# Vector 5 of layer 0 weighed by VectorE, routing in fewer operations, and one expert's share of a gate quarter placed in the second gather buffer

## The reference, cut to what matters

```python
c_act = jax.nn.silu(c)
for layer in range(DEPTH):
    mod = c_act @ w_ada[layer] + b_ada[layer]
    sh1, sc1, g1, sh2, sc2, g2 = jnp.split(mod[:, None, :], 6, axis=-1)
    h = rmsnorm(x, mix_norm_g[layer]) * (1.0 + sc1) + sh1
    ...
g_idx = jnp.argmax(g_logits, axis=-1).astype(jnp.int32)
top_v, top_i = lax.top_k(e_logits, TOP_K)
e_w = jax.nn.softmax(top_v, axis=-1) * g_w[:, None]
...
def expert_block(args):
    xb, e = args
    return (jax.nn.silu(xb @ w_gate[e]) * (xb @ w_up[e])) @ w_down[e]
```

## Time and profile before

| | us |
|---|---|
| median of 3 runs | 1225.13 (1224.36 to 1225.23) |
| the profiled execution's own time | 1224.53 |
| its span, first to last instruction | 1222.8 |
| TensorE busy, VectorE busy | 885.8, 359.5 |
| mean granted TensorE clock | 0.877 of full speed |
| moved by DMA over the span | 490.06 MB, mean 401 GB/s |

### The profile page before, as it was taken

One profiled execution on the slowest core, in us unless ns is written; L12 is line 12 of the kernel. 1 busy time (PEld: TensorE's weight loads), 2 busy tenths in 40 slices (PEclk: granted clock), 3 DMA queues, 4 the chain that ended last, 5 costly groups with the idle time before them and its releaser, 6 DMA issues.

```text
span 1222.8 us, 14486 instructions
## 1 busy us (share of the span) xinstructions
PE 885.8 (72%) x5988; PEld 428.3 (35%) x5988; DVE 359.5 (29%) x900; ACT 169.7 (14%) x400; POOL 23.1 (2%) x67
## 2 busy tenths in 40 slices
PE   6999998647474756656699999976566665665647
PEld 5867453222231212121278554532121212121212
DVE  3298545121111111111124587521111111202111
ACT  1124331000000000000033253400000000000000
POOL 1001100000000000000000100000000000000000
PEclk9999999878887868787899999998787878877888
DMA  9999999999999999999996849799999999999997
GB/s 346 396 401 408 410 406 423 424 428 427 428 428 428 429 428 429 428 427 428 401 409 256 336 191 379 291 419 428 428 428 428 428 428 429 428 429 429 427 426 290
DMA packets 64249, 490.06 MB, mean 401 GB/s; under 512 B 5664, under 2 KB 8113, under 8 KB 39616
## 3 DMA queue, kind: packets, MB, share of 16 engines
q1 hardware_dynamic: 61680, 486.56, 96.1%
q10 hardware_dynamic: 2512, 2.69, 0.6%
HBM read 488.18 MB, written 1.05 MB: 400 GB/s over the span
## 4 chain that ended last, share of the span: by engine, by line
DMA 51%; PE 40%; DVE 3%; SPq 3%; ACT 1%; issue 1%; POOL 0%; DVEq 0%; ACTq 0%
PE psum L1663 40%; DMA weight_ring<-in_moe_w_down 18%; DMA weight_ring<-in_moe_w_gate 17%; DMA weight_ring<-in_moe_w_up 14%; SPq L496 2%; DMA weight_ring<-in_w_ada 1%; SPq L525 1%; DVE h_or_mix_T L1138 0%; PE psum L1759 0%; DVE h_or_mix_T L1404 0%; ACT phase_region L912 0%; DVE phase_region L1614 0%; ACT phase_region L1039 0%; DVE phase_region L1108 0%; DVE phase_region L1225 0%
## 5 line engine op out<-in xcount | busy, mean ns | idle before, releaser
L1663 PE MATMUL psum<-weight_ring,h_or_mix_T 128*32 128x512 f32 (+1 forms) x2240 | 381.7, 705 | 228.0 <-DMA weight_ring<-in_moe_w_gate 134.8
L1663 PEld LDWEIGHTS psum<-weight_ring,h_or_mix_T 128*32 128x32 f32 (+1 forms) x2240 | 119.2, 135 | 472.5 <-issue 470.0
L1663 PE MATMUL psum<-weight_ring,ada_partials 128*32 128x512 f32 (+1 forms) x1088 | 140.2, 671 | 81.1 <-DMA weight_ring<-in_moe_w_down 76.0
L1663 PE MATMUL psum<-phase_region 128*128 128x128 f32 (+5 forms) x824 | 155.4, 350 | 4.3 <-DVE x_tokens L1389 1.3
L1663 PEld LDWEIGHTS psum<-phase_region 128*128 128x128 f32 (+2 forms) x824 | 99.6, 188 | 77.4 <-issue 57.2
L1663 PE MATMUL psum<-h_or_mix_T,weight_ring 128*128 128x256 f32 (+1 forms) x528 | 115.0, 376 | 2.9 <-DVE h_or_mix_T L1138 2.7
L1663 PEld LDWEIGHTS psum<-h_or_mix_T,weight_ring 128*128 128x128 f32 x528 | 96.6, 190 | 20.3 <-issue 4.4
L1663 PEld LDWEIGHTS psum<-weight_ring,ada_partials 128*32 128x32 f32 x1088 | 40.7, 125 | 170.9 <-issue 161.2
L1458 DVE TENSOR_TENSOR phase_region<-psum,gate_rows 128x512 f32<-128x512 f32 x28 | 19.4, 692 | 207.7 <-PE psum L1663 207.7
L1447 DVE SCALAR_TENSOR_TENSOR ada_partials<-phase_region,psum 128x512 f32<-128x512 f32 x16 | 16.8, 1051 | 211.3 <-PE psum L1663 211.3
L1442 DVE SCALAR_TENSOR_TENSOR phase_region<-phase_region,psum 128x512 f32<-128x512 f32 x16 | 11.0, 687 | 228.0 <-ACT phase_region L945 228.0
(11 more groups left out here) (217 smaller groups left out, 469.9 us busy)
## 6 DMA issues: line engine op xcount, KB each, us to landing
weight_ring<-in_moe_w_up SPq DMA_DIRECT2D x64, 2048.0 KB, 20.1
weight_ring<-in_moe_w_gate SPq DMA_DIRECT2D x62, 2048.0 KB, 20.2
weight_ring<-in_moe_w_down SPq DMA_DIRECT2D x60, 2048.0 KB, 19.8
weight_ring<-in_w_ada SPq DMA_DIRECT2D x10, 3072.0 KB, 20.4
weight_ring<-in_odd_w_in SPq DMA_DIRECT2D x6, 2048.0 KB, 23.2
weight_ring<-in_w_ada SPq DMA_DIRECT2D x10, 1024.0 KB, 22.6
weight_ring<-in_w_ada SPq DMA_DIRECT2D x4, 2048.0 KB, 17.7
weight_ring<-in_even_w_in SPq DMA_DIRECT2D x3, 2048.0 KB, 21.1
```

Source lines behind the costliest of these rows:

```text
L1663: return pe.matmul(out_, lhsT, rhs, start=first, stop=last, **kw)
```

## The change

Three parts, in both layers unless said otherwise.

**Vector 5.** `modulation_sums(5, ...)`, the copy and `gate_join(5)` go. VectorE weighs the eight row blocks of the slab (`weigh_gate`, one operation of 128x1024 each) in five places of its program, and TensorE adds over the partitions with two matmuls (`add_gate_rows`) after the router's. SyncE's waits follow. Around it the convolution's centring, squares and sums are moved forward on VectorE, ScalarE and TensorE. Layer 0 only.

**Routing.** The comparisons read the integer indices directly, without a cast ahead of them; two one-hot operations and an addition become one operation of twice the width, which TensorE reads as it is, in twice as many matmuls.

**The share.** Gate quarter 1 is loaded for three experts. The fourth's share (512 KB) goes to `ASIDE`, which is `XT[:, 1]`, once the router's matmuls are done; the quarter of a down matrix (512 KB) whose place this leaves free is loaded right behind, and only the other 1.5 MB wait for `first_quarters`.

```diff
+        ASIDE = XT[:, 1, :, :].rearrange("p k q -> p (k q)")
...
+                kept = WIDE - 1 if (k, half) == (0, 1) else WIDE
+                sp.dma_start(by_quarter(EXTRA if first else region(n, half))[:, 0:kept],
+                             gate_src[L, :, 0:kept, at:at + QUARTER]).then_inc(extra_in if first else filled(n, half), 16)
...
                 if L == 0:
+                    sp.wait_ge(gate_weighted, KD // 2)
+                    load_first(3, 1)
                     sp.wait_ge(out_half, 1)
                     load_first(2, 1)
-                    sp.wait_ge(ada_half, 1)
-                    load_first(3, 1)
+                    sp.wait_ge(gate_weighted, KD)
+                    load_first(4, 0)
                     sp.wait_ge(wout_done, 4)
                     load_first(3, 0)
-                    sp.wait_ge(ada_summed, sums_by(5))
-                    load_first(4, 0)
...
+                n, rows = MOE0[L] + 4, by_quarter(region(MOE0[L] + 4, 1))
+                sp.wait_ge(logits_done, L + 1)
+                sp.dma_start(ASIDE, gate_src[L, :, WIDE - 1, QUARTER:2 * QUARTER]).then_inc(extra_in, 16)
+                sp.dma_start(rows[:, KF - 1], down_src[L, :, 1, (KF - 1) * D:KF * D]).then_inc(filled(n, 1), 16)
                 sp.wait_ge(first_quarters, 3 * L + 1)
-                load_unit(L, 4, 1, 0)
+                sp.dma_start(rows[:, 0:KF - 1], down_src[L, :, 1, 0:(KF - 1) * D].rearrange("p (k n) -> p k n", k=KF - 1)
+                             ).then_inc(filled(n, 1), 16)
...
+            def add_gate_rows():
+
+                pe.wait_ge(gate_weighted, KD)
+                for half in range(2):
+                    ins = mm(PS[:, (6, JOIN_BANK[5])[half], :], ONES[:, :], GATE_ROWS[:, half * HALF:(half + 1) * HALF], True, True)
+                ins.then_inc(gate_summed, 1)
...
-            modulation_sums(5, 0, KD // 2)
             pe.wait_ge(conv_out, 1)
...
-                    modulation_sums(5, KD // 2, KD)
+                    add_gate_rows()
                     keep_warm(1, 5)
                 else:
-                    pe.wait_ge(router_ready, 2 * L + 2)
                     add_rows(11)
-                    keep_warm(1, 8)
+                    keep_warm(1, 5)
...
+                        if part == 1:
+                            pe.wait_ge(extra_in, 16 * (4 + 2 * L))
+                            experts[-1] = ASIDE
...
-                if L == 0:
-                    gate_join(5)
-                else:
-                    keep_warm(1, 9)
+                keep_warm(1, 8)
```

More of the change, by code:

```diff
@@ L383, in landed @@
             return 16 * sum(home(m, h) == home(n, half) for m in range(n + 1) for h in range(2)
-                            if (m, h) <= (n, half) and not (m in MOE0 and h == 0))
+                            if (m, h) <= (n, half) and not (m in MOE0 and h == 0)
+                            for part in range(2 if (m - 4 in MOE0 and h == 1) else 1))
         def occupant(n):
@@ L1255, in _, with weigh_gate @@
             ins.then_inc(conv_centred, 1)
-            take_modulation(4)
+            floor_logs(3)
             dve.wait_ge(conv_squared, 1)
             add_blocks(CSQ)
+            take_modulation(4)
+            def weigh_gate(lo, hi):
+                s = slab_index("ada", 5)
+                for k in range(lo, hi):
+                    if k == 0:
+                        dve.wait_ge(slab_in[SPOT[s]], landed(s, 0))
+                        ins = v.tensor_scalar(GATE_ROWS, wide(s)[:, k, :], CCOL[:, 1, k:k + 1], None, ALU.mult)
+                    else:
+                        if k == ADA_FIRST:
+                            dve.wait_ge(rest_in[SPOT[s]], landed(s, 1))
+                        dve.wait_ge(gate_weighted, k)
+                        ins = v.scalar_tensor_tensor(out=GATE_ROWS, in0=wide(s)[:, k, :], scalar=CCOL[:, 1, k:k + 1],
+                                                     in1=GATE_ROWS, op0=ALU.mult, op1=ALU.add)
+                    ins.then_inc(gate_weighted, 1)
+            weigh_gate(0, 1)
             dve.wait_ge(conv_rstd, 1)
@@ L1355, in moe @@
                 dve.wait_ge(rank_done, L + 1)
-                for s in range(2):
-                    ins = v.tensor_tensor(ONEHOT[:, s, :, :], ONEHOT[:, s, :, :],
-                                          PS[:, 7, P:P + TB * NE].rearrange("p (t n) -> p t n", t=TB), ALU.mult)
-                link(ins)
+                dve.wait_ge(onehot_ready, L + 1)
+                link(v.tensor_tensor(ONEHOT[:, :, :, :], CHOSEN[:, :, :, :],
+                                     PS[:, 7, P:P + TB * NE].rearrange("p (t n) -> p t n", t=TB).unsqueeze(1)
+                                     .broadcast_to([P, 2, TB, NE]), ALU.mult))
                 link(v.tensor_reduce(RANK.rearrange("p t s -> p s t"), ONEHOT[:, 0:2, :, :], AX.X, ALU.add))
@@ L1977, in moe @@
                 ins.then_inc(logits_done, 1)
+                pe.wait_ge(router_ready, 2 * L + 2)
                 if L == 0:
[L1979 removed]
+                    add_gate_rows()
                     keep_warm(1, 5)
                 else:
[L1982 removed]
                     add_rows(11)
[L1984 removed]
+                    keep_warm(1, 5)
                 pe.wait_ge(onehot_ready, L + 1)
[L1987 to L1993 removed]
+                for t in range(TB):
+                    at = slice(P + t * NE, P + (t + 1) * NE)
+                    for s in range(2):
+                        ins = mm(PS[:, 7, at], BEFORE[:, :], CHOSEN[:, s, t, :], s == 0, s == 1 and t == 0,
+                                 skip_group_check=True)
+                for s in range(2):
+                    ins = mm(PS[:, 7, at], ALL[:, :], CHOSEN[:, s, 0, :], False, s == 1, skip_group_check=True)
+                ins.then_inc(rank_done, 1)
+                for s in range(2):
+                    for t in range(TB):
+                        ins = mm(PS[:, 0, 0:NE], ALL[:, :], CHOSEN[:, s, t, :], s + t == 0, s + t == 2,
+                                 skip_group_check=True)
+                ins.then_inc(counted, 1)
                 def gather(buf, done):
@@ L2049, in widen_first @@
                         pe.wait_ge(arrived, land)
+                        experts = [w[:, e] for e in range(WIDE)]
+                        if part == 1:
+                            pe.wait_ge(extra_in, 16 * (4 + 2 * L))
+                            experts[-1] = ASIDE
                         for k in (2 * part, 2 * part + 1):
@@ L2053, in widen_first @@
                                 ins = mm(PS[e * SLOT:(e + 1) * SLOT, 0, :], xt[:, k, e * SLOT:(e + 1) * SLOT],
-                                         w[:, e, k % 2 * F:(k % 2 + 1) * F], n == 0 and k % 2 == 0, n == 3 and k % 2 == 1,
+                                         experts[e][:, k % 2 * F:(k % 2 + 1) * F], n == 0 and k % 2 == 0, n == 3 and k % 2 == 1,
                                          skip_group_check=True)
```

79 lines of the change are left out of this document (33 added, 46 removed).

## The result

The changed kernel's median is 1232.53 us (1229.47 to 1235.87, 7 executions), that of the kernel before in the same comparison 1225.13: a ratio of 1.0058, with a 95% interval of 1.0048 to 1.0067. It is slower by 7.4 us. The forecast was 1228.1, slower by 3.0; the time lies outside its range. The profiled execution took 1230.23 (span 1228.4), 5.7 more than the profiled one of before; so the trace shows 5.7 of the 7.4.

The account below looks back on a forecast made before the run. The DMA engines were taken to bound the kernel, with layer 0's queue all but dry at the release and a gap in layer 1. Layer 0 +4.9 and layer 1 -1.9 gave +3.0 on 1225.13, 1228.1 us; range 1224.5 to 1230.5.

Parts of the forecast that it names:

- layer 0's share: Layer 0: share lands at 180.1 behind a full queue, first quarter waits and runs at half clock; costs 4.9 us.
- the fifty matmuls: Layer 0, TensorE: 32 records fewer at 146.24 and again at 167.85, part of vector 5's change, costed at nothing.
- Which resource sets the end, and the share's place in the queue: DMA engines set the end; layer 0's share, queued in order, lands at 180.1, so the release is 6.1 us later.
- The rival that the share overtakes what is ahead of it: Layer 0: share lands by about 176 and costs nothing, layer 1 gains 1.9; time 1222.9, chance 0.17.
- Less the 1.2 us of bytes already moved, the rest of layer 0's stream runs 4.9 us later: Layer 0: release 6.1 us later, credited 1.2 us for the early down quarter; bounds 3.4 and 6.1.
- the rival of a second gap: Layer 0: later refills of the first quad come 1.2 us closer to the queue's end, credit lost; 1229.3, chance 0.07.
- Vector 5 and the reordering "at nothing": Layer 0 before the first quarter: costs nothing, since the DMA backlog until 178 or later covers several microseconds either way.
- the first dent: Layer 0, 177 to 180: DMA at 289 of 429 GB/s over 3 us; closing it gains 1.0 us at most.
- Layer 1: Layer 1: routing 0.7 us earlier plus 1.2 us of down quarter moved into the gap; gains 1.9, bounds 0.4 to 2.3.

Follow-up runs that it names:

- the shifted changed kernel: Changed kernel plus 25 two-column matmuls on TensorE in layer 0's second quad, where it waits for the DMA engines: 1230.67 us, 1.0038 to before.
- the 25 matmuls in the wait: Changed kernel plus 25 two-column matmuls on TensorE in layer 0, between the gather and the wait for the share: 1230.16 us, 1.0040 to before.
- layer 1's share alone with the shift: Changed kernel, share in layer 1 only, plus 25 two-column matmuls in layer 0's second quad: 1221.73 us, 0.9972 to before.
- three pairs of kernels: Layer 1's share only, no share, and changed, each without and with 25 matmuls in layer 0's second quad: 1224.25/1221.73, 1225.45/1222.50, 1233.36/1230.67 us.
- 7.89 us in one kernel: Changed kernel, share in layer 1 only, plus 25 two-column matmuls behind layer 0's first gather, with no wait to hide them: 1230.01 us.
- sixty-two of those: Records of 31 further warming matmuls added to the changed kernel in layer 0, between the gather and the wait for the share: 1226.19 us.

## Why the prediction was wrong

The forecast was +3.0, measured were +7.4. Two terms of the sum failed: layer 0's share was put at +4.9 and costs 6.8 in the medians, and the fifty matmuls that the change takes away were put at nothing and cost some 2.7. What follows goes through the prediction in its own order.

*Which resource sets the end, and the share's place in the queue: right.* The share landed at 180.2 (forecast 180.1), TensorE idled 7.85 us (some 7), the clock was 0.50, the first quarter ended at 183.7 (183.5), and the DMA engines stood still behind it (5 GB/s from 180.5 to 183). The rival that the share overtakes what is ahead of it is dead: 14.4 us in the queue in layer 0, against 6.8 in layer 1, where less was ahead. The Trainium skill ("DMA: Bandwidth & Descriptors", section "Anatomy of one DMA") has, for a transfer on another issuing path, a price that gives an estimate of 2.0 + 1.57 MB / 436 GB/s = 5.6 us for the transfer released into the empty queue; it took 6.5 in both layers.

*"Less the 1.2 us of bytes already moved, the rest of layer 0's stream runs 4.9 us later": too small.* The first transfer behind the release was indeed 4.89 later (190.21 against 185.32). But by the third 0.8 of the credit was gone, 5.65 (201.57 against 195.93). In size this is two thirds of the rival of a second gap; a gap is not to be seen, for from 195 to 201.6 the DMA engines moved 418 GB/s. The third release is issued at 190.11, 5.0 us before the transfer ahead of it lands at 195.08, and lands 6.5 us after that one; before, the distance was 7.1 (183.87 to 190.99), and it landed 4.9 us after, which is what its bytes take. In the profile of the shifted changed kernel the same transfer is 6.8 later. In two other kernels the credit stayed whole: with the 25 matmuls in the wait the release is 5.6 later than before and this transfer 4.2, with the share alone put into the kernel before 6.7 and 5.4. So the loss is not in each execution, and why it comes is open.

*Vector 5 and the reordering "at nothing", because the backlog covers it in either direction: wrong, though it did not show in the changed kernel.* Without the share in layer 0 the first quarter ended 3.1 us earlier (release at 174.40), and that was worth 1.5 us of the stream: a transfer near its end lands at 598.21 and not at 599.71. In the three other profiles with vector 5 changed, no share in layer 0 and no work added ahead of the quarter it is 1.8 to 2.4 us. The reader could have seen it in the earlier trace rows, where the dent of 289 GB/s says that the queue is already too short at 177. Columns as in the earlier trace rows; first before, then layer 1's share alone with the shift:

```profile
175.00:180.00 5.00, 4.63 (x40) 2.12 (x42) 1.32 (x6) 0.92 (x2) 0.00 (x0) 1.00 0.95 354
205.00:215.00 10.00, 5.77 (x56) 1.87 (x48) 3.89 (x13) 0.00 (x0) 0.00 (x0) 1.00 0.99 400
```
```profile
175.00:180.00 5.00, 4.63 (x40) 2.20 (x43) 0.82 (x2) 0.92 (x2) 0.00 (x0) 1.00 1.04 431
205.00:215.00 10.00, 5.68 (x54) 3.67 (x46) 3.21 (x13) 0.00 (x0) 0.00 (x0) 0.78 1.00 426
```

(431 - 354) x 5 / 431 = 0.9 us and (426 - 400) x 10 / 426 = 0.6. I had bounded the first dent at 1.0 and not looked for a second. So the share in layer 0 costs its delay and also this gain: 1230.67 less 1221.73, 8.9 us between two kernels that differ in nothing else. Their two profiled executions are 11.0 apart (1232.08 less 1221.09), of which the pieces seen make 9.9: 6.8 at the end of layer 0's stream, 1.5 of the gain given up, 1.6 at 745. The last 1.1 comes behind layer 1's third release and was not followed.

*Layer 1: right.* Forecast -1.9, measured -0.7 for routing and -1.05 for the bytes, -1.75. TensorE waited at most 0.15 us for the share there, since the transfer ahead of it took 10.2 us and not 8.4; it was just in time. The one operation that replaces the one-hot pair and the addition took 0.29, estimated at 0.30:

```profile
781.52 0.29 DVE L1379 TENSOR_TENSOR expert_chosen<-expert_number,expert_index 128x128 bf16<-128x128 f32 x1
...
782.22 0.29 DVE L1388 TENSOR_TENSOR expert_onehot<-expert_chosen,psum 128x128 f32<-128x128 bf16 x1
```

*The fifty matmuls less, put at nothing: wrong, and the largest single miss.* The change takes fifty matmul records off TensorE (5988 before, 5938 after; 47 of them ahead of the boundary), and I counted them as saved time only. They are also places by which everything behind them moves, and that cost 1.5 us in each profiled execution, more where the clock fell behind it, and about 2.7 in the medians of three pairs of kernels (2.5, 2.95, 2.7). In the DMA view of the changed kernel from 624.0 to 625.5, just as TensorE falls still, two packets of another kind are on their way:

```profile
q8 instruction: 1, 0.02, 4.5%
q14 instruction: 1, 0.01, 1.4%
```

The packets of this kind on the first queue have 16,384 bytes; this one starts at 624.0, the smaller one on the second at 625.3, and the idle is from 624.8 to 626.4. Before has such a pair at 618.4 and 619.7, around the same transposes, and no idle. The rows do not say for which engine a packet is. The Trainium skill ("Runtime: NRT & Kernel Launch", section "Instruction fetch mechanics") says that an engine's instructions come in blocks of 16 KiB, 256 instructions, that crossing from one to the next is mostly hidden, and that a taken branch to a place outside of what is loaded stalls. The size agrees with the trace, and a block's edge that moves with the count agrees with the runs; that a branch behind layer 0's experts leaves the fetch too late here would follow from its rule, and no run here tests it. Shown is that the idle depends on the number of instructions ahead; that it is a fetch is argued.

The account for the medians: layer 0 +6.8 (forecast +4.9; this is 1230.94 less 1224.19, the share alone), the boundary +2.7 (nothing), layer 1 -1.75 (-1.9; from the profile), together +7.75 against the 7.4 measured. Of the 1.9 by which layer 0 was put too low a part is in its stream, which ends 5.3 to 6.8 later than before in the five profiles whose first quarter waits for the share until 179 or later and then runs at half clock; 1.6 more comes at 745 in some of them. How often each happens, and so how the 1.9 divides, is open. Putting back the number of instructions does not rescue the forecast: 1230.67 is still 5.7 above before.

## What to carry to other kernels

An early transfer that shares a queue is early only by what stands ahead of it: in layer 1 the same share is worth 0.8 us in the median (1222.50 to 1221.73, intervals that overlap), in layer 0, behind a full queue, it costs 6.8 in the kernel before and 8.9 in the changed one. A dent in a row of bandwidth says that the engine ahead is already waited for there, so a faster or slower stage before it is not to be counted as free. And where an edit takes instructions away, look in the trace far behind it for idle time without a releaser before its result is put down to the edit.

## What the runs showed that I had not expected

- TensorE stands 1.6 to 1.8 us in mid-sequence with no releaser in the five profiles of the four kernels that have fifty records less than before, and in none of the others, which have the number of before or more. Behind it the clock stayed up in two of the five (the 56 records at 12.35) and fell in three (13.97, 14.04, 14.82), the changed kernel among the first and among the second.
- Fifty matmul records of two columns with 128 by 128 weights took 7.89 us in one kernel and 6.54 in another, 158 and 131 ns each, no less than records of 128 columns: sixty-two of those took 7.09, 114 ns each. The granted clock fell to 0.50 between 175 and 177 while TensorE worked through the fifty without a pause, so part of their time is at half clock, and the sixteen records of 512 columns behind them took 3.64; over the sixty-two it stayed at 1.00, and those behind them ran at full speed.
- Behind the same idle of 1.7 us near 740 the granted clock fell to 0.50 in some profiles and not in others.
